# Latent attention with queries and keys made channels-first, and the three passes of a 256-column block in one sum

## The chip, the cores and the metric

The kernel runs on one core of a Trainium2 chip. The metric is the device time of one execution in microseconds (us). TensorE multiplies, VectorE (DVE) and ScalarE (ACT) work element by element, GpSimd (POOL) does a few small things, and the queue of SP issues the loads. Three runs of the kernel before took 1927.31, 1927.44 and 1927.97 us.

## The reference

Two networks run one after the other on 256 tokens of 2048 channels, in float32. The first has two layers, each with a differential attention of 8 heads and a latent attention (MLA) of 8 heads; only the latter is touched. Cut to what matters:

```python
q_b = jnp.einsum('bsr,re->bse', _rms_norm(c_q, mla_q_norm_g[l]), w_uq[l])      # rank 512 -> 8 * (128 + 64)
q_nope, q_rope = q_b[..., :128], q_b[..., 128:]                                # per head
kv = jnp.einsum('bsr,re->bse', _rms_norm(c_kv, mla_kv_norm_g[l]), w_ukv[l])    # rank 512 -> 8 * (128 + 128)
k_nope, v_b = kv[..., :128], kv[..., 128:]
s = (einsum('bqhd,bkhd->bhqk', q_nope, k_nope) + einsum('bqhr,bkr->bhqk', q_rope, k_rope)) * scale
s = jnp.where(dist >= 0, s, NEG_INF); p = softmax(s); o = einsum('bhqk,bkhd->bqhd', p, v_b)
```

## The kernel before

**Products in two parts.** Every weight matrix comes from memory in units of 128 x 1024 numbers (4 KB a partition). ScalarE rounds a unit to its high part (`round_unit`, L393), VectorE takes the rest (`rest_unit`, L398), and TensorE makes three passes for each tile: high by high, high by rest, rest by high. Units go through a ring of four slots; ScalarE and VectorE prepare unit u + 3 in their step u. `product_rows` (L420, passes on L435 to L437) holds a tile of activations (128 channels x 128 tokens) as weights of the array and moves 512 columns of the weight matrix past it, 12 passes a unit; tokens come out on the partitions. `product_cols` (L440), used in the second network only, holds the weight tile and moves tokens: 8 passes of 512 columns (L458, high and rest of the activations side by side) and 8 of 256 (L451).

**Banks.** Sums of a chunk (one block of output columns) lie in a pair of PSUM banks; chunk c uses pair c % 2. `banks_free` (L481) lets TensorE start chunk c when the chunk two before has been copied out, and `evacuated` (L486) lets others wait for that copy. Who copies counts up `acc_free`.

**One layer** has 56 units for q, k, v and gate of the differential attention, then 32 units here called the latent stage (loops at L1261, L1689, L2116), 32 units of the gate of the latent attention (the gate stage, `z_heads`), and 32 of the output matrix. In the latent stage units 0 to 7 and 8 to 15 make the two latents c_q and c_kv (chunks 6 and 7), 16 and 17 the rope key (chunk 8, `product_rope_key`), 18 to 23 the queries (chunks 9 to 11, two units each), 24 to 31 keys and values (chunks 12 to 15).

**Head work is written between the units.** In the latent stage head h of the differential attention has units 4h to 4h + 3: behind unit 4h TensorE turns the weights of the head before (L1115) and q and k of head h (`turn`, L510); behind unit 4h + 1 it multiplies the outputs (L1121 to L1123) and the scores (L1134). ScalarE's list in these steps: copies of the turned weights and of the turned q and k (L1604, L1591), the output of the head (L1611, L1615), the exponentials (L1597). VectorE's list: `diff_max` in step 4h + 1 (L1995 to L2002), `diff_weights` in step 4h + 3 (L2008 to L2014). Every engine works through its list in order, so a wait holds back all that is behind it.

**The latents.** They are scaled by the rms of the tokens and turned to channels-first (`C_TURN`: behind units 10 and 11 for c_q, 18 and 19 for c_kv). ScalarE sums their squares in steps 8 and 16, VectorE makes 1/rms of both by `rsqrt` (eleven small operations, L557 to L562) in step 19, and ScalarE multiplies by it when it copies the products out (L1719). VectorE's `key_sum` (L2119, L2120), at the head of step 18, adds the two halves of the rope key and frees its pair.

**The latent heads** run in the gate stage. Behind unit 4h + 2 TensorE turns the queries and keys without position of head h (`mla_block`, L1167, eight turns of four blocks a layer), ScalarE copies them to `qkT`, and behind unit 4h + 3 `mla_scores` (L1145) multiplies them and adds the rope part. GpSimd rotates the queries' rope part (L1013 to L1019) when chunks 10 and 11 are copied, and TensorE turns it behind the first unit of the gate stage.

## Time and profile before

| what | value |
|---|---|
| median of three runs | 1927.44 us |
| profiled execution | 1927.67 us |
| its span, first to last instruction | 1925.9 us |
| TensorE busy | 1915.0 us, 99% |
| VectorE busy | 1432.9 us, 74% |
| ScalarE busy | 1082.4 us, 56% |
| GpSimd busy | 46.3 us, 2% |
| granted TensorE clock, mean | 0.999 of full speed |

The profiled execution's own time is 1.8 us longer than its span; sums are made against it. Matmuls are pipelined: a pass of 512 columns has a duration of 0.39 us in the list while the next one starts 0.23 us later, so the time that a pass takes up is read from the distance between starts. Layer 0 has its latent stage from about 187 to 287 us and its gate stage from 287 to about 376 us; layer 1 repeats the pattern about 442 us later.

### The profile page before, as it was taken

How to read it: one execution, taken by the hardware profiler on the slowest of the kernel's cores; microseconds unless marked ns; L12 is line 12 of the kernel's file. 1: busy time of each engine (PE TensorE's matmuls, PEld its weight loads, DVE VectorE, ACT ScalarE, POOL GpSimd, SP SyncE). 2: the span in 40 equal slices, each digit the busy share in tenths (PEclk: the TensorE clock that was granted, in tenths of full speed). 3: DMA queues.
4: the chain of work that ended last, by engine and by line, in shares of the span. 5: the costliest groups of instructions: out<-in, count | busy, mean ns of one | idle time of the engine just before them, and what ended most of it. 6: DMA issues, size and time to landing. Idle time of an engine off the chain costs nothing.

```text
span 1925.9 us, 26620 instructions
## 1 busy us (share of the span) xinstructions
PE 1915.0 (99%) x9721; PEld 1624.3 (84%) x9721; DVE 1432.9 (74%) x2059; ACT 1082.4 (56%) x1598; POOL 46.3 (2%) x74
## 2 busy tenths in 40 slices
PE   9999999999999999999999999999999999999998
PEld 7888888888888888888888888888888888888886
DVE  7777675656777675656767766888878887889898
ACT  6555686655545676654644444555555555555554
POOL 1000030000000030000100000000000000000000
PEclk9999999999999999999999999999999999999999
DMA  9864455565665456455666455665666656666664
GB/s 345 309 209 131 147 154 155 152 204 188 209 208 165 141 162 177 142 164 186 210 186 195 154 165 185 185 186 178 203 185 188 192 185 187 191 222 193 203 195 164
DMA packets 248058, 361.29 MB, mean 188 GB/s; under 512 B 15504, under 2 KB 134496, under 8 KB 247456
## 3 DMA queue, kind: packets, MB, share of 16 engines
q1 hardware_dynamic: 246112, 353.15, 58.3%
q0 software_dynamic: 1568, 6.60, 1.0%
q8 instruction: 57, 0.93, 0.2%
q10 hardware_dynamic: 288, 0.33, 0.0%
q14 instruction: 33, 0.27, 0.0%
HBM read 356.88 MB, written 3.16 MB: 187 GB/s over the span
## 4 chain that ended last, share of the span: by engine, by line
PE 97%; DVE 1%; DMA 1%; ACT 0%; issue 0%; SPq 0%; DVEq 0%; ACTq 0%
PE acc L458 22%; PE acc L451 12%; PE acc L435 11%; PE acc L437 11%; PE acc L436 11%; PE acc L1204 4%; PE acc L1205 4%; PE acc L1203 4%; PE acc L1467 3%; PE acc L1465 3%; PE acc L1466 3%; PE aux L515 2%; PE aux L1134 1%; PE aux L1467 1%; PE aux L1465 1%; PE aux L1466 1%
## 5 line engine op out<-in xcount | busy, mean ns | idle before, releaser
L398 DVE TENSOR_TENSOR sb_w_lo<-sb_stage,sb_w_hi 128x1024 fp32r<-128x1024 f32 x476 | 583.1, 1227 | 273.1 <-ACT sb_w_hi L393 266.5
L393 ACT ACTIVATE sb_w_hi<-sb_stage 128x1024 fp32r<-128x1024 f32 x476 | 502.3, 1058 | 349.6 <-PE acc L451 123.0
L458 PE MATMUL acc<-sb_xT,sb_w_hi 128*128 128x512 f32 x1856 | 445.7, 391 | 0.0
L458 PEld LDWEIGHTS acc<-sb_xT,sb_w_hi 128*128 128x128 f32 x1856 | 340.8, 188 | 65.8
L451 PEld LDWEIGHTS acc<-sb_xT,sb_w_lo 128*128 128x128 f32 x1856 | 238.7, 191 | 9.3
L451 PE MATMUL acc<-sb_xT,sb_w_lo 128*128 128x256 f32 x1856 | 243.0, 283 | 0.0
L435 PE MATMUL acc<-sb_w_hi,sb_mT 128*128 128x512 f32 x544 | 217.3, 399 | 0.0
L437 PE MATMUL acc<-sb_w_hi,sb_mT 128*128 128x512 f32 x544 | 212.2, 390 | 0.0
L436 PE MATMUL acc<-sb_w_lo,sb_mT 128*128 128x512 f32 x544 | 212.1, 390 | 0.0
L435 PE MATMUL acc<-sb_w_hi,sb_xT 128*128 128x512 f32 x384 | 155.9, 406 | 0.0
L437 PE MATMUL acc<-sb_w_hi,sb_xT 128*128 128x512 f32 x384 | 150.0, 391 | 0.0
L436 PE MATMUL acc<-sb_w_lo,sb_xT 128*128 128x512 f32 x384 | 149.9, 390 | 0.0
L435 PEld LDWEIGHTS acc<-sb_w_hi,sb_mT 128*128 128x128 f32 x544 | 102.2, 188 | 22.5 <-issue 1.0
L437 PEld LDWEIGHTS acc<-sb_w_hi,sb_mT 128*128 128x128 f32 x544 | 102.2, 188 | 22.0
L436 PEld LDWEIGHTS acc<-sb_w_lo,sb_mT 128*128 128x128 f32 x544 | 102.3, 188 | 19.7
L1203 PE MATMUL acc<-sb_w_hi,sb_xT 128*128 128x512 f32 x220 | 85.7, 389 | 0.0
L1205 PE MATMUL acc<-sb_w_hi,sb_xT 128*128 128x512 f32 x220 | 85.6, 389 | 0.0
L1204 PE MATMUL acc<-sb_w_lo,sb_xT 128*128 128x512 f32 x220 | 85.6, 389 | 0.0
L437 PEld LDWEIGHTS acc<-sb_w_hi,sb_xT 128*128 128x128 f32 x384 | 72.1, 188 | 15.7
L435 PEld LDWEIGHTS acc<-sb_w_hi,sb_xT 128*128 128x128 f32 x384 | 72.2, 188 | 13.9
L738 ACT ACTIVATE sb_w_hi<-sb_pair_stage 128x1024 fp32r<-128x1024 f32 (+1 forms) x50 | 48.3, 982 | 62.2 <-DVE sb_pair_stage L751 53.1
L436 PEld LDWEIGHTS acc<-sb_w_lo,sb_xT 128*128 128x128 f32 x384 | 72.3, 188 | 12.7
(437 smaller groups left out, 2872.6 us busy)
## 6 DMA issues: line engine op xcount, KB each, us to landing
sb_stage<-w_in SPq DMA_DIRECT2D x232, 512.0 KB, 4.1
sb_stage<-w_up SPq DMA_DIRECT2D x176, 512.0 KB, 3.9
sb_stage<-w_out SPq DMA_DIRECT2D x96, 512.0 KB, 4.0
sb_stage<-w_down SPq DMA_DIRECT2D x54, 512.0 KB, 6.8
sb_pair_stage<-w_down SPq DMA_DIRECT2D x34, 512.0 KB, 5.4
sb_kvb<-w_in SPq DMA_DIRECT2D x16, 512.0 KB, 6.2
sb_stage<-w_ukv SPq DMA_DIRECT2D x16, 512.0 KB, 3.8
sb_stage<-w_kv SPq DMA_DIRECT2D x15, 512.0 KB, 6.2
```

What stands on the lines that cost most here:

```text
L393: act.activation(w_hi[:, j % RING, 0:size], stage[:, j % RING, 0:size], ACT.Copy).then_inc(hi_ready, 1)
L398: dve.tensor_tensor(w_lo[:, j % RING, 0:size], stage[:, j % RING, 0:size], w_hi[:, j % RING, 0:size].bitcast(F32), ALU.subtract).then_inc( ...
L435: pe.matmul(o, x_hi, hi[:, k, :], start=first and k == 0, stop=False)
L436: pe.matmul(o, x_hi, lo[:, k, :], start=False, stop=False)
L437: mm = pe.matmul(o, x_lo, hi[:, k, :], start=False, stop=last and k == nk - 1)
L451: mm = pe.matmul(acc[:, 2 * pair + c, 0:SEQ], lo[:, k, c * P:(c + 1) * P], xT[:, k0 + k, 0, :], start=False, stop=False)
L458: mm = pe.matmul(acc[:, 2 * pair + c, :], hi[:, k, c * P:(c + 1) * P], both, start=first and k == 0, stop=last and k == 3)
L1203: pe.matmul(o, a(0), hi, start=start, stop=False)
L1204: pe.matmul(o, a(0), lo, start=False, stop=False)
L1205: return pe.matmul(o, a(1), hi, start=False, stop=stop)
L1465: pe.matmul(o, a(0), hi, start=start, stop=False)
L1466: pe.matmul(o, a(0), lo, start=False, stop=False)
```

## The change

Queries and keys without position are now made channels-first. `w_uq` and `w_ukv` are put together anew on the host, the 128-wide parts of all heads first and the rope or value parts behind them. Units 18 to 21 hold all 512 latent channels by 256 query columns (two heads each), units 24 to 27 the same for keys. The new `product_latent_cols` holds weight tiles and moves the 256 tokens past them: for each of 4 x 2 tiles three passes of 256 columns, all into the same sum. Each of these units is a chunk of its own. Units 22 and 23 make the rope parts of the queries and 28 to 31 the values, as rows, as before.

The turns of the eight latent heads and their copies are gone; `mla_scores` reads the copied chunks. Since tokens no longer lie on the partitions there, 1/rms of c_q goes into the scores' scale (`query_scale`), and c_kv is multiplied by its 1/rms before it is turned (ScalarE, step 18). For that the `rsqrt` stands in VectorE's step 17, and the turns of c_kv behind units 19 and 21. ScalarE copies a column chunk at the head of the step behind it, and the row chunks in steps 24, 30 and the first of the gate stage.

```diff
+DIFF_TB = [2, 3, 4, 7, 8, 10, 12, 13]
+C_TURN = {10: (0, 0, 5), 11: (0, 1, 6), 19: (1, 0, 9), 21: (1, 1, 11)}
...
+QUERY_COLS, KEY_COLS = {18 + n: n for n in range(4)}, {24 + n: n for n in range(4)}
+C_QUERY, C_ROPE, C_KEY, C_VALUE, C_Z, C_OUT = 9, 13, 14, 18, 20, 24
...
+        def product_latent_cols(pe, base, j, k0, pair):
+
+
+            pe.wait_ge(lo_ready, base + (j + 1))
+            hi, lo = (w[:, j % RING, :].rearrange("p (k n) -> p k n", n=256) for w in (w_hi, w_lo))
+            tiles = [(k, c) for k in range(4) for c in range(2)]
+            for k, c in tiles:
+                o, cols = acc[:, 2 * pair + c, 0:SEQ], slice(c * P, (c + 1) * P)
+                pe.matmul(o, hi[:, k, cols], mT[:, k0 + k, 0, :], start=k == 0, stop=False)
+                pe.matmul(o, hi[:, k, cols], mT[:, k0 + k, 1, :], start=False, stop=False)
+                mm = pe.matmul(o, lo[:, k, cols], mT[:, k0 + k, 0, :], start=False, stop=k == 3)
+            mm.then_inc(unit_used, 1)
...
+        query_pair = lambda n: qb[:, n % 2, n // 2 * 512:(n // 2 + 1) * 512].rearrange("p (h t) -> p h t", h=2)
+        key_pair = lambda n: kvb[:, 0, n * 512:(n + 1) * 512].rearrange("p (h t) -> p h t", h=2)
+        query_of, key_of = (lambda h: query_pair(h // 2)[:, h % 2, :]), (lambda h: key_pair(h // 2)[:, h % 2, :])
+        value_of = lambda h, t: kvb[:, 1, t * WIDTH + h * DV:t * WIDTH + (h + 1) * DV]
+        output_of = lambda h, t: kvb[:, 0, h * SEQ + t * DV:h * SEQ + (t + 1) * DV]
+        rope_rows = lambda t: qb[:, t, WIDTH:WIDTH + HEADS * ROPE]
...
-                    for c in range(3):
+                    for n in range(4):
+                        load(sp, base, U_QKV + 18 + n, rows(w_uq, 4, 0, 4, n * 256, 256), 256)
+                    for i in range(2):
+                        load(sp, base, U_QKV + 22 + i, rows(w_uq, 4, i, 2, WIDTH), 512)
+                    for n in range(4):
+                        load(sp, base, U_QKV + 24 + n, rows(w_ukv, 4, 0, 4, n * 256, 256), 256)
+                    for c in range(2):
                         for i in range(2):
-                            load(sp, base, U_QKV + 18 + 2 * c + i, rows(w_uq, 4, i, 2, c * 512), 512)
-                    for c in range(4):
-                        for i in range(2):
-                            load(sp, base, U_QKV + 24 + 2 * c + i, rows(w_ukv, 4, i, 2, c * 512), 512)
+                            load(sp, base, U_QKV + 28 + 2 * c + i, rows(w_ukv, 4, i, 2, WIDTH + c * 512), 512)
...
-                    evacuated(pool, pairs, 10)
-                    evacuated(pool, pairs, 11)
+                    evacuated(pool, pairs, C_ROPE)
...
-                        pe.wait_ge(tb_free, tb0 + (MLA_TB[h] + 1))
+                        if h == 0:
+                            evacuated(pe, pairs, C_KEY + 2)
+                            evacuated(pe, pairs, C_KEY + 3)
+                            pe.wait_ge(tb_free, tb0 + QR_TB + 2)
+                            pe.wait_ge(pv_free, pv0 + 2 * HEADS)
                         pe.wait_ge(row_max, head0 + (HEADS + h))
                         for col, q, keys in ((0, 1, SEQ), (SEQ, 0, P)):
                             o = sc1[:, col:col + keys]
-                            pe.matmul(o, qkT[:, q * P:(q + 1) * P], qkT[:, 2 * P:2 * P + keys], start=True, stop=False)
+                            pe.matmul(o, query_of(h)[:, q * P:(q + 1) * P], key_of(h)[:, 0:keys], start=True, stop=False)
                             mm = pe.matmul(o, qrT[:, h // 2, q * P:(q + 1) * P], krz[:, h % 2, 0:keys],
...
-                            if h < HEADS:
-                                turn(pe, tb0 + MLA_TB[h], mla_block(h))
...
+                        c, i = u // 8, u % 8
+                        if u >= 18:
+                            c, i = C_ROPE - 6, u - 22
+                            if u in QUERY_COLS:
+                                c, i = C_QUERY - 6 + QUERY_COLS[u], 0
+                            if u in KEY_COLS:
+                                c, i = C_KEY - 6 + KEY_COLS[u], 0
+                            if u >= 28:
+                                c, i = C_VALUE - 6 + (u - 28) // 2, u % 2
...
+                        elif u in QUERY_COLS or u in KEY_COLS:
+                            product_latent_cols(pe, base, U_QKV + u, 0 if u < 24 else 4, c % 2)
...
+                            if j == 1:
+                                pe.wait_ge(ckv_scaled, layer + 1)
...
+                    def copy_cols(u, chunk, dst):
+
+                        multiplied(act, quads * 4, U_QKV + u)
+                        pair = chunk % 2
+                        act.activation(dst, acc[:, 2 * pair:2 * pair + 2, 0:SEQ], ACT.Copy).then_inc(acc_free[pair], 1)
+
+                    def copy_rows(u, chunk, dst):
+
+                        multiplied(act, quads * 4, U_QKV + u)
+                        for t in range(T):
+                            ins = act.activation(dst(t), acc[:, 2 * (chunk % 2) + t, :], ACT.Copy)
+                        ins.then_inc(acc_free[chunk % 2], 1)
+
+                    value_rows = lambda c: lambda t: kvb[:, 1, t * WIDTH + c * 512:t * WIDTH + (c + 1) * 512]
+
                     for u in range(32):
+                        if u - 1 in QUERY_COLS:
+                            copy_cols(u - 1, C_QUERY + QUERY_COLS[u - 1], query_pair(QUERY_COLS[u - 1]))
+                        if u - 1 in KEY_COLS:
+                            copy_cols(u - 1, C_KEY + KEY_COLS[u - 1], key_pair(KEY_COLS[u - 1]))
                         rounded(U_QKV + u)
+                        if u == 18:
+                            act.wait_ge(c_rstd, layer + 1)
+                            for t in range(T):
+                                ckv = qb[:, t, RANK:2 * RANK]
+                                ins = act.activation(ckv, ckv, ACT.Copy, scale=rstd_c[:, T + t:T + t + 1])
+                            ins.then_inc(ckv_scaled, 1)
...
-                        if u == 20 or (u > 20 and u % 2 == 1):
-                            c = (u - 19) // 2
-                            act.wait_ge(c_rstd, layer + 1)
-                            multiplied(act, quads * 4, U_QKV + 19 + 2 * c)
-                            for t in range(T):
-                                r = (0 if c < 3 else T) + t
-                                dst = qb[:, t, c * 512:(c + 1) * 512] if c < 3 else \
-                                    kvb[:, t, (c - 3) * 512:(c - 2) * 512]
-                                ins = act.activation(dst, acc[:, 2 * ((9 + c) % 2) + t, :], ACT.Copy,
-                                                     scale=rstd_c[:, r:r + 1])
-                            ins.then_inc(acc_free[(9 + c) % 2], 1)
+                        if u == 24:
+                            copy_rows(23, C_ROPE, rope_rows)
+                        if u == 30:
+                            copy_rows(29, C_VALUE, value_rows(0))
                     for u in range(32):
+                        if u == 0:
+                            copy_rows(31, C_VALUE + 1, value_rows(1))
...
-                        dve.tensor_scalar(s[:, 0:P], sc1[:, 0:P], MLA_SCALE, None, ALU.mult)
-                        two = lambda ap: ap.rearrange("p (m k) -> p m k", m=2)
-                        step(dve.scalar_tensor_tensor(out=two(s[:, P:3 * P]), in0=two(sc1[:, P:3 * P]), scalar=MLA_SCALE,
-                                                      in1=again(causal[:, :], 2), op0=ALU.mult, op1=ALU.add))
+                        dve.scalar_tensor_tensor(out=s[:, 0:SEQ], in0=sc1[:, 0:SEQ], scalar=query_scale[:, 1:2],
+                                                 in1=causal[:, :], op0=ALU.mult, op1=ALU.add)
+                        step(dve.scalar_tensor_tensor(out=s[:, SEQ:SEQ + P], in0=sc1[:, SEQ:SEQ + P],
+                                                      scalar=query_scale[:, 0:1], in1=causal[:, P:2 * P],
+                                                      op0=ALU.mult, op1=ALU.add))
...
-                        if u == 19:
+                        if u in (19, 21):
...
+                        if u == 17:
+                            dve.wait_ge(c_squared, layer * 4 + 4)
+                            rsqrt(step, dve, rstd_c[:, :], sumsq_c[:, :], 4, RANK, done=c_rstd)
+                        if u == 20:
+                            dve.wait_ge(c_rstd, layer + 1)
+                            step(dve.tensor_scalar(query_scale[:, :], rstd_c[:, 0:T], MLA_SCALE, None, ALU.mult))
                         if u % 4 == 1:
                             diff_max(u // 4)
-                        if u == 19:
-                            dve.wait_ge(c_squared, layer * 4 + 4)
-                            rsqrt(step, dve, rstd_c[:, :], sumsq_c[:, :], 4, RANK, done=c_rstd)
...
+    by_part = lambda name, first: np.asarray(arrays[name]).reshape(LAYERS, RANK, HEADS, -1)[:, :, :, first]\
+        .reshape(LAYERS, RANK, -1)
+    data["w_uq"] = np.concatenate([by_part("w_uq", slice(0, NOPE)), by_part("w_uq", slice(NOPE, NOPE + ROPE))], axis=2)
+    data["w_ukv"] = np.concatenate([by_part("w_ukv", slice(0, NOPE)), by_part("w_ukv", slice(NOPE, NOPE + DV))], axis=2)
```

VectorE before, from the rest of unit 20 (step 17, L398) over the scores' maximum of head 4 (L1995 to L2002) to `key_sum` (L2119, L2120) and the rest of unit 21:

```order
L398 TENSOR_TENSOR sb_w_lo<-sb_stage,sb_w_hi 128x1024 [waits hi_ready]
L1995 SCALAR_TENSOR_TENSOR sb_s<-aux,sb_bias 128x512 [waits scores_ready]
L1997 SCALAR_TENSOR_TENSOR sb_s<-aux,sb_bias 128x256
L2000 TENSOR_REDUCE sb_neg_max<-sb_s 128x2 [waits dve_step]
L2001 TENSOR_REDUCE sb_neg_max<-sb_s 128x2
L2002 TENSOR_SCALAR sb_neg_max<-sb_neg_max 128x4 [waits dve_step]
L2119 COPY sb_qb<-acc 128x256 [waits unit_used]
L2120 TENSOR_TENSOR sb_qb<-acc,sb_qb 128x256 [waits dve_step]
L398 TENSOR_TENSOR sb_w_lo<-sb_stage,sb_w_hi 128x1024 [waits hi_ready]
```
VectorE in the changed kernel, the same place (L572 to L577 is the `rsqrt`, L2038 to L2045 the maximum, L2163 and L2164 `key_sum`):

```order
L400 TENSOR_TENSOR sb_w_lo<-sb_stage,sb_w_hi 128x1024 [waits hi_ready]
L572 TENSOR_SCALAR sb_newton_v<-sb_sumsq_c 128x4 [waits c_squared]
...
L577 SCALAR_TENSOR_TENSOR sb_rstd_c<-sb_newton_t,sb_rstd_c 128x4 [waits dve_step]
L2038 SCALAR_TENSOR_TENSOR sb_s<-aux,sb_bias 128x512 [waits scores_ready]
L2040 SCALAR_TENSOR_TENSOR sb_s<-aux,sb_bias 128x256
L2043 TENSOR_REDUCE sb_neg_max<-sb_s 128x2 [waits dve_step]
L2044 TENSOR_REDUCE sb_neg_max<-sb_s 128x2
L2045 TENSOR_SCALAR sb_neg_max<-sb_neg_max 128x4 [waits dve_step]
L2163 COPY sb_qb<-acc 128x256 [waits unit_used]
L2164 TENSOR_TENSOR sb_qb<-acc,sb_qb 128x256 [waits dve_step]
L400 TENSOR_TENSOR sb_w_lo<-sb_stage,sb_w_hi 128x1024 [waits hi_ready]
```
The eleven operations of `rsqrt` have come in between the rest of unit 20 and the maximum, and so ahead of `key_sum`.

ScalarE before, from the exponentials of head 5 (L1597, step 22) on; L393 rounds a unit, L1719 copies queries, L1604 and L1591 are the copies behind unit 24's head work:

```order
L1597 ACTIVATE sb_s,sb_row_sum<-sb_s,sb_neg_max 128x128 x2
L393 ACTIVATE sb_w_hi<-sb_stage 128x1024 [waits unit_used,staged2]
L1719 ACTIVATE sb_qb<-acc,sb_rstd_c 128x512 [waits unit_used,c_rstd]
L1719 ACTIVATE sb_qb<-acc,sb_rstd_c 128x512
L393 ACTIVATE sb_w_hi<-sb_stage 128x1024 [waits unit_used,staged3]
L1604 ACTIVATE sb_pT<-aux 128x384 [waits pv_filled]
L1591 ACTIVATE sb_turn_f<-aux 128x512 [waits tb_filled]
L393 ACTIVATE sb_w_hi<-sb_stage 128x1024 [waits unit_used,staged0]
```
ScalarE in the changed kernel; L1722 copies the rows of units 22 and 23 (chunk 13), L1716 the columns of unit 24:

```order
L1624 ACTIVATE sb_s,sb_row_sum<-sb_s,sb_neg_max 128x128 x2
L395 ACTIVATE sb_w_hi<-sb_stage 128x1024 [waits unit_used,staged2]
L395 ACTIVATE sb_w_hi<-sb_stage 128x1024 [waits unit_used,staged3]
L1631 ACTIVATE sb_pT<-aux 128x384 [waits pv_filled]
L1618 ACTIVATE sb_turn_f<-aux 128x512 [waits tb_filled]
L1722 ACTIVATE sb_qb<-acc 128x512 [waits unit_used]
L1722 ACTIVATE sb_qb<-acc 128x512
L1716 ACTIVATE sb_kvb<-acc 128x512 [waits unit_used]
L395 ACTIVATE sb_w_hi<-sb_stage 128x1024 [waits unit_used,staged0]
```
The copy of units 22 and 23 stood ahead of the rounding in step 23, and now stands behind the two copies that wait for the head work of unit 24.

## Rows read from the trace of the kernel before

**Rows 1.** The page: busy time by engine (share of the span), and the chain's shares
```profile
PE 1915.0 (99%) x9721; PEld 1624.3 (84%) x9721; DVE 1432.9 (74%) x2059; ACT 1082.4 (56%) x1598; POOL 46.3 (2%) x74
...
PE 97%; DVE 1%; DMA 1%; ACT 0%; issue 0%; SPq 0%; DVEq 0%; ACTq 0%
```
**Rows 2.** Timeline of TensorE, a turn alone: start us, duration us, instruction, count
```profile
216.35 0.60 PE L515 MATMUL aux<-sb_ident,sb_qb 128*128 128x128 f32 x4
216.71 0.48 PE L435 MATMUL acc<-sb_w_hi,sb_xT 128*128 128x512 f32 x1
217.03 0.39 PE L436 MATMUL acc<-sb_w_lo,sb_xT 128*128 128x512 f32 x1
```
**Rows 3.** Timeline of TensorE, row products: first and last of 24 passes in a row
```profile
270.58 0.39 PE L435 MATMUL acc<-sb_w_hi,sb_mT 128*128 128x512 f32 x1
...
275.80 0.40 PE L437 MATMUL acc<-sb_w_hi,sb_mT 128*128 128x512 f32 x1
```
**Rows 4.** Timeline of TensorE, a head's turn behind the turn of its weights
```profile
395.05 0.38 PE L515 MATMUL aux<-sb_ident,sb_qb 128*128 128x128 f32 x2
395.27 0.38 PE L515 MATMUL aux<-sb_ident,sb_kvb 128*128 128x128 f32 x2
395.41 0.48 PE L435 MATMUL acc<-sb_w_hi,sb_xT 128*128 128x512 f32 x1
```
**Rows 5.** Timeline of TensorE, column products of the second network's first part
```profile
1244.83 2.08 PE L451 MATMUL acc<-sb_xT,sb_w_lo 128*128 128x256 f32 x16
1246.74 3.82 PE L458 MATMUL acc<-sb_xT,sb_w_hi 128*128 128x512 f32 x16
```
**Rows 6.** The page, weight loads of these 256-column passes: busy us, mean ns
```profile
L451 PEld LDWEIGHTS acc<-sb_xT,sb_w_lo 128*128 128x128 f32 x1856 | 238.7, 191 | 9.3
```
**Rows 7.** Timeline of TensorE, first pass of unit 18 (layer 0)
```profile
239.49 0.50 PE L435 MATMUL acc<-sb_w_hi,sb_mT 128*128 128x512 f32 x1
```
**Rows 8.** Timeline of VectorE, units 17 to 20 of layer 0
```profile
240.44 0.69 DVE L1995 SCALAR_TENSOR_TENSOR sb_s<-aux,sb_bias 128x512 f32<-128x512 f32 x1
...
242.62 0.42 DVE L2119 COPY sb_qb<-acc 128x256 f32<-128x256 f32 x1
...
243.41 1.22 DVE L398 TENSOR_TENSOR sb_w_lo<-sb_stage,sb_w_hi 128x1024 fp32r<-128x1024 f32 x1
...
250.00 0.16 DVE L557 TENSOR_SCALAR sb_newton_v<-sb_sumsq_c 128x4 f32<-128x4 f32 x1
...
252.05 1.22 DVE L398 TENSOR_TENSOR sb_w_lo<-sb_stage,sb_w_hi 128x1024 fp32r<-128x1024 f32 x1
```
**Rows 9.** Timeline of ScalarE, the last of the exponentials of head 4
```profile
244.43 0.19 ACT L1597 ACTIVATION_READ_ACCUMULATOR sb_s<-sb_s,sb_neg_max 128x1 f32 x1
```
**Rows 10.** Timeline of TensorE, head work behind unit 24, and unit 25
```profile
262.60 0.49 PE L1115 MATMUL aux<-sb_ident,sb_s 128*128 128x128 f32 x3
...
263.28 0.48 PE L435 MATMUL acc<-sb_w_hi,sb_mT 128*128 128x512 f32 x1
```
**Rows 11.** Timeline of ScalarE, the copies of that head, and of a chunk
```profile
263.12 0.49 ACT L1604 ACTIVATE sb_pT<-aux 128x384 f32<-128x384 f32 x1
...
264.06 1.05 ACT L393 ACTIVATE sb_w_hi<-sb_stage 128x1024 fp32r<-128x1024 f32 x1
...
268.49 1.27 ACT L1719 ACTIVATE sb_kvb<-acc,sb_rstd_c 128x512 f32<-128x512 f32 x2
...
269.64 1.07 ACT L393 ACTIVATE sb_w_hi<-sb_stage 128x1024 fp32r<-128x1024 f32 x1
```
**Rows 12.** Timeline of GpSimd, first and last operation of the queries' rotation
```profile
262.40 1.53 POOL L1013 TENSOR_TENSOR sb_kz<-sb_qb,sb_rope 128x512 f32<-128x512 f32 x1 [0.90 <-ACT sb_qb L1719]
...
273.68 0.80 POOL L1019 TENSOR_TENSOR sb_kz<-sb_kz 128x256 f32<-128x256 f32 x1
```
**Rows 13.** Timeline of TensorE, the start of the program
```profile
1.02 5.06 PE L1050 MATMUL acc<-sb_turn_f 128*128 128x128 f32 x22 [1.02 <-POOL sb_turn_f L960]
...
5.82 1.19 PE L1060 MATMUL acc<-sb_w_hi,sb_mT 128*128 128x512 f32 x2
```

More of the change, by code:

```diff
@@ L79 @@
 N_FFN = D_FF // 256
-C_MEM, C_LAYER = 2, 24
+C_MEM, C_LAYER = 2, 28
 G_NORM = 0
@@ L223, in shape_constants @@
     q, k = np.arange(P)[:, None], np.arange(P)[None, :]
-    causal = np.where(q - k >= 0, 0.0, NEG).astype(np.float32)
+    causal = np.concatenate([np.zeros((P, P)), np.where(q - k >= 0, 0.0, NEG)], axis=1).astype(np.float32)
     inv = (1.0 / (THETA ** (np.arange(0, ROPE, 2, dtype=np.float32) / ROPE))).astype(np.float32)
@@ L1177, in gated_block @@
                             return lambda i: qa[:, t, (4 * g + i) * DV:(4 * g + i + 1) * DV]
-                        v = lambda i: (4 * (g - 2) + i) * (NOPE + DV)
-                        return lambda i: kvb[:, t, v(i):v(i) + DV]
+                        return lambda i: output_of(4 * (g - 2) + i, t)
                     def z_heads(u):
                         h, r = (u - 2) // 4, (u - 2) % 4
-                        if u >= 2 and r == 0:
-                            if 0 < h <= HEADS:
-                                mla_turn_weights(h - 1)
-                            if h < HEADS:
-                                turn(pe, tb0 + MLA_TB[h], mla_block(h))
+                        if u >= 2 and r == 0 and 0 < h <= HEADS:
+                            mla_turn_weights(h - 1)
                         if u >= 2 and r == 1:
@@ L1627, in mla_output @@
                         act.wait_ge(pv_filled, pv0 + (2 * HEADS + 2 * h + 2))
-                        v = h * (NOPE + DV)
                         for t, col, r in ((1, 0, 0), (0, P, 1)):
-                            ins = act.activation(kvb[:, t, v:v + DV], pv[:, col:col + P], ACT.Copy,
+                            ins = act.activation(output_of(h, t), pv[:, col:col + P], ACT.Copy,
                                                  scale=inv_sum[:, r:r + 1])
@@ L1636, in z_heads @@
                         h, r = (u - 2) // 4, (u - 2) % 4
-                        if u >= 2 and r == 0:
-                            if 0 < h <= HEADS:
-                                copy_weights(2 * HEADS + 2 * (h - 1))
-                            if h < HEADS:
-                                copy_bank(MLA_TB[h], qkT)
+                        if u >= 2 and r == 0 and 0 < h <= HEADS:
+                            copy_weights(2 * HEADS + 2 * (h - 1))
                         if u >= 2 and r == 1 and 0 < h <= HEADS:
@@ L2042, in gate_outputs @@
                             dve.wait_ge(pv_free, layer * (4 * HEADS) + (2 * HEADS + 8 * (g - 1)))
-                            o = kvb[:, t, :].rearrange("p (h e) -> p h e", h=HEADS)[:, 4 * (g - 2):4 * (g - 1), 0:DV]
+                            o = kvb[:, 0, :].rearrange("p (h t d) -> p h t d", h=HEADS, t=T)[:, 4 * (g - 2):4 * (g - 1), t, :]
                         dve.tensor_tensor(o, o, z, ALU.mult).then_inc(gated, 1)
```

59 lines of the change are left out of this document (24 added, 35 removed).

## The prediction

> **What bounds the kernel now.** I read the page first. TensorE is busy 99% of the span and carries 97% of the chain that ended last [rows 1]. So nothing that only VectorE, ScalarE or GpSimd does costs time, unless it makes TensorE wait; and every pass that TensorE is spared or given counts in full. I then took the timeline of TensorE through one layer, to price a pass and a turn by the distance between starts (durations overlap, so a row's duration is no price), and the timelines of VectorE and ScalarE around the latent units, to see when each sum is copied out of its pair of banks. In the document's numbering the stage has units 0 to 31. Both layers show the same pattern, so I work out layer 0 and double.
>
> **Turns removed.** Eight turns of four 128-column passes go per layer. A turn standing alone: start at 216.35, next product at 216.71, and that product's first pass takes 0.32 to the next start where 0.227 is usual [rows 2, 3]. That is 0.36 + 0.09 = 0.45 us. Seven of the eight stand behind the turn of a head's weights, whose tail is paid anyway; they give 395.05 to 395.41 = 0.36 us each [rows 4]. Together 0.45 + 7 x 0.36 = 2.97 us a layer. One of the two turns of the normalized key latent moves from behind unit 18 to behind unit 21, where scores stand before it: another 0.09. What they removed on ScalarE (a copy per head) was hidden under TensorE's products and gives nothing.
>
> **Passes.** A row product has 12 passes of 512 columns, a unit of the new kind 24 of 256: the same columns, twice the instructions. 512 columns: 23 distances from 270.58 to 275.80, 0.227 each [rows 3], so 2.72 us a unit. 256 columns, each with weights of its own, stand in the mixer's column products: 16 from 1244.83 to 1246.74, 0.1194 each [rows 5], so 2.87 us a unit. The price is 0.14 us for each of eight units, 1.1 us a layer. Bounds: half of 0.227 would make it nothing; if a weight load, 191 ns long in its rows [rows 6], could not lie under the pass before it, a unit would take 24 x 0.191 = 4.58, 1.86 more. I take 0.1194, since in rows 5 the weights change at every pass as here. Not shown there is three passes in a row into the same 256 columns of a bank; the 512-column passes of rows 3 do that without a gap, so I add nothing.
> The Trainium skill, "TensorE: Matmul & The Clock Gate", says under "The mechanism" (Part 3) that a weight load overlaps a running matmul only where the row groups differ. By that rule every one of these passes would pay its load; rows 5 and 6 contradict it (16 starts in 1.91 us with loads of 191 ns), and the measurement decides.
>
> **First new wait: unit 19 for the sum of the rope key.** This is where I expect the saving to go. Each query block is now a chunk of its own, so unit 18 takes pair 1 and unit 19 already pair 0, in which the rope key of units 16 and 17 lies until VectorE's key_sum has read it. Before, pair 0 was wanted only by unit 20. At the same time the rsqrt of the latents is moved ahead of diff_max(4) and key_sum on VectorE (the order shown in the section on the change).
> Without a wait unit 19 would start at 239.49 [rows 7] + 0.09 tail + 2.87 = 242.45. VectorE is through with the rest of unit 20 at 240.44. The rsqrt takes 250.00 to 252.05, 2.05 us, so 242.49. diff_max(4) took 240.44 to 242.62, 2.18, so 244.67. key_sum took 242.62 to 243.41, 0.79, so 245.46 [rows 8]. TensorE then loads weights, 0.19 [rows 6], and starts at 245.65. A wait of 3.2 us per layer. Behind it stand the turn of the key latent, unit 20 and head 4's weights; none has another way past. What is late next: ScalarE's exponentials of head 4 wait for diff_max, and the copy that frees pair 1 for unit 20 stands behind them. They ended at 244.43 + 0.19, 2.0 after diff_max [rows 8, 9]; so now at 246.7, and with half of a chunk's 1.15 [rows 11] the copy at 247.3. Unit 20 wants it at 245.65 + 2.87 + 0.36 = 248.9. No wait there.
>
> **Second new wait: unit 25 for the rope part of the queries.** Units 22 and 23 are a row chunk in pair 1, unit 24 a chunk in pair 0, and unit 25 wants pair 1 again. The copy of units 22 and 23 stands on ScalarE behind unit 24's head work: the copy of the turned weights and the copy of the turned q and k, both of which wait for TensorE after unit 24. From rows: TensorE's head work behind unit 24 began at 262.60, the next product at 263.28; ScalarE had both copies done at 264.06, that is 1.46 after the head work began. The two 512-column copies of a chunk took 268.49 to 269.64, 1.15 [rows 10, 11]. So the pair is free 2.61 after the head work's start, with a weight load 2.80, where unit 25 would start at 0.68: 2.1 us a layer. This one doesn't depend on how late anything runs before, since ScalarE waits for TensorE itself and TensorE for ScalarE.
>
> **What else moves.** GpSimd starts the queries' rotation after that copy instead of after the one at 262; it took 262.40 to 273.68 + 0.80 [rows 12] and is wanted only behind the first unit of the gate stage, which begins at 287, so even 7 us later it is hidden. Scaling the key latent on ScalarE (two copies) comes before head 4's exponentials, which wait longer for diff_max anyway: nothing. The two operations of mla_max become two others of like size, the loads have the same bytes in other blocks; SP issues as many, and nothing waits for a load: nothing. The copy of the first value chunk now stands behind head 7's exponentials and is wanted by the first unit of the gate stage; I take nothing for it and put up to 1 us on the upper side, together with the slowing of VectorE beside GpSimd's rotation.
>
> **Sum.** Per layer: -2.97 - 0.09 + 1.1 + 3.2 + 2.1 = +3.4 us. Twice: +6.8. The profiled execution took 1927.67 (span 1925.9, 1.8 around it), which makes 1934.5; it lies 0.23 above the median of the runs, so in their terms 1934.2. I forecast 1934.4, slower by 0.36%.
>
> **Rivals.** A difference under 0.2% (3.9 us) can't be told from none here.
> - The saving stands and the waits do not: another release comes earlier than I read. -2.97 - 0.09 + 1.1 = -1.9 a layer, 1923.6, which is at the edge between "same" and "faster". For it: TensorE hardly ever waits before. Against: both waits follow from the order on a single queue. With only the first wait left it would be 1930, with only the second 1927.9. 8% for none, 8% for one.
> - TensorE's clock falls in the gaps. The granted clock is at full speed in all 40 slices of before, and no gap of 3 us stands in the trace after the start. At the start, behind idle time, 22 passes of 128 columns took from 1.02 to 5.82, 0.218 each, where two such passes now take 395.05 to 395.27, 0.110 each: 2.4 us lost [rows 4, 13]. If that came once per layer, 1939.2. 8%. The Trainium skill, the same page, "What's actually happening", says that the array's clock is at half by default and released by activity, so that idle time lets it fall again; no row here shows it behind a gap like this one.
> - Passes of 256 columns cost the length of a weight load: 16 x 1.86 = 29.8 in place of 2.3 makes 1962. 3%.
> The forecast has 73%, with a range of its own from 1932 to 1937. Taking in one lost wait and the clock, the range is 1929.8 to 1939.8. Slower: 73 + 8 + 3, less 2 for a forecast that comes out smaller than the bound, 0.82. The 8 for one wait, those 2 and 2 of the 8 for none are same, 0.12; the other 6 are faster, 0.06.
>
> **What will show it.** In the profile after: TensorE idle for about 3.2 us ahead of the first 256-column pass of the second query block in each layer, released by VectorE's key_sum, and about 2.1 us ahead of the second key block, released by ScalarE's copy; both in the list of waits as two occurrences each. The turn group of qb and kvb has 64 fewer passes. 24 starts of the new line in 2.87 us. The gate stage is shorter by about 3 us a layer. I am wrong if TensorE's idle time stays near 2 us, if the granted clock shows less than full speed in the slices of the latent units, or if the new passes start over 0.125 apart.

## The result, and the profile after

| | median, us | runs | range, us |
|---|---|---|---|
| before | 1928.13 | 6 | 1927.31 to 1930.62 |
| after | 1936.70 | 6 | 1935.77 to 1937.65 |

The ratio is 1.0043, with a 95% interval of 1.0032 to 1.0054: slower, as forecast, and 2.3 us above the forecast time. The profiled execution took 1936.7 us with a span of 1934.9, 9.0 more than the one of before.

Look first at the list of what TensorE waited for. Its columns are engine and line, the releaser, then us in total, times, and the longest.

```profile
PE acc L480 <- DVE sb_qb L2164: 6.0, 2, 3.0
PE acc L480 <- ACT sb_qb L1722: 3.3, 2, 1.7
PE acc L1551 <- DVE sb_w_lo L767: 1.2, 1, 1.2
```

L480 is the first pass of a block of query or key channels. L2164 is VectorE's key_sum and L1722 is ScalarE's copy of units 22 and 23. Both waits are the forecast ones, once per layer each. The third is at the very end of the program, where before it showed 0.3 (there the line is L1524).

The page says the same of the whole: TensorE is still busy 99% of the span, but its part of the chain that ended last fell from 97% to 94% and VectorE's rose to 3%, answering to [rows 1].

```profile
PE 1913.7 (99%) x9849; PEld 1628.4 (84%) x9849; DVE 1433.8 (74%) x2061; ACT 1074.9 (56%) x1586; POOL 47.3 (2%) x74
...
PE 94%; DVE 3%; ACT 1%; DMA 1%; issue 1%; SPq 0%; ACTq 0%; DVEq 0%
```

TensorE's timeline in layer 0, first passes of unit 18, its last shown pass, and the start of unit 19 (start us, duration us, instruction, count, idle time before it and its releaser):

```profile
239.66 0.39 PE L480 MATMUL acc<-sb_mT,sb_w_hi 128*128 128x256 f32 x1
239.88 0.28 PE L481 MATMUL acc<-sb_mT,sb_w_hi 128*128 128x256 f32 x1
...
242.40 0.28 PE L481 MATMUL acc<-sb_mT,sb_w_hi 128*128 128x256 f32 x1
242.52 0.28 PE L482 MATMUL acc<-sb_mT,sb_w_lo 128*128 128x256 f32 x1
245.79 0.39 PE L480 MATMUL acc<-sb_mT,sb_w_hi 128*128 128x256 f32 x1 [2.99 <-DVE sb_qb L2164]
...
266.62 0.54 PE L1138 MATMUL aux<-sb_ident,sb_s 128*128 128x128 f32 x3
...
269.26 0.39 PE L480 MATMUL acc<-sb_mT,sb_w_hi 128*128 128x256 f32 x1 [1.67 <-ACT sb_qb L1722]
```

The new passes start 0.12 apart. Unit 19 could have started at 242.64 and starts at 245.79: 3.15 us. The head work behind unit 24 starts at 266.62 and unit 25 only 2.64 later, where it was 0.68 in [rows 10]: 1.96 us. The bracket shows less than the start-to-start loss, because it counts idle time from the modelled end of the last pass. Distances between starts are what the kernel pays.

VectorE ahead of unit 19 shows why: the rsqrt, diff_max(4) and key_sum stand one behind the other.

```profile
240.63 0.16 DVE L572 TENSOR_SCALAR sb_newton_v<-sb_sumsq_c 128x4 f32<-128x4 f32 x1
...
242.69 0.68 DVE L2038 SCALAR_TENSOR_TENSOR sb_s<-aux,sb_bias 128x512 f32<-128x512 f32 x1
...
244.86 0.42 DVE L2163 COPY sb_qb<-acc 128x256 f32<-128x256 f32 x1
...
245.65 1.22 DVE L400 TENSOR_TENSOR sb_w_lo<-sb_stage,sb_w_hi 128x1024 fp32r<-128x1024 f32 x1
```

Key_sum is through at 245.65, read as in [rows 8] by the start of the operation behind it; the forecast had 245.46 and unit 19 at 245.65.

**Where the 9.0 us are.** I compare the starts of the head work (L1115 before, L1138 after). From the one behind unit 16 to the one behind the first unit of the gate stage, layer 0 took 54.21 us before (235.25 to 289.46) and takes 60.47 now (235.44 to 295.91): +6.26. The two waits are 5.11 of it, eight units at 0.14 are 1.14, the moved turn gives 0.04 back, together 6.21. From there to the last head's weights it was 118.93 and is 115.71: -3.22, the turns. (These weights are turned behind the third unit of the output stage. The gate stage itself runs from 286.7 to 400.1 us in the kernel before, not to 376.) So layer 0 pays 3.04. Layer 1 pays 3.05 of the same kind and 1.49 more, because there TensorE's clock fell. The wait at the very end is 0.9 longer. That is 8.5 of 9.0. Of the rest, 0.19 in each layer lie between the head work behind unit 4 and that behind unit 16 (40.30 us before, 40.49 now). TensorE has the same 211 passes and turns there in both kernels, but 116 of the row passes start 229.7 ns apart on average where it was 227.8.

The clock in layer 1, by stretches of 1 us (stretch, length, busy time and count of TensorE, its weight loads, VectorE, ScalarE and GpSimd, granted clock, DMA share, GB/s):

```profile
689.00:690.00 1.00, 0.00 (x0) 0.00 (x0) 0.96 (x4) 0.15 (x2) 0.00 (x0) 1.00 0.00 0
690.00:691.00 1.00, 0.25 (x2) 0.25 (x3) 0.97 (x3) 1.00 (x5) 0.00 (x0) 1.00 0.00 0
691.00:692.00 1.00, 1.00 (x8) 1.00 (x8) 0.99 (x2) 1.00 (x6) 0.00 (x0) 0.73 0.00 0
692.00:693.00 1.00, 1.00 (x7) 1.00 (x6) 0.93 (x4) 1.00 (x2) 0.00 (x0) 0.50 0.06 15
...
694.00:695.00 1.00, 1.00 (x7) 1.00 (x7) 0.00 (x0) 0.00 (x0) 0.00 (x0) 0.56 0.62 204
695.00:696.00 1.00, 1.00 (x11) 1.00 (x10) 0.14 (x1) 0.00 (x0) 0.00 (x0) 1.00 0.00 0
```

TensorE was idle for 3.0 us up to 690.75. About 0.7 us after it went on, the granted clock fell to 0.50, which is the lower of its two levels (1.2 GHz), and came back before 695. The passes between stand 0.21 apart instead of 0.12 (692.49, 692.70, 692.91, 693.13 in the timeline). In the 40 slices of the page nothing of it can be seen: every slice of the granted clock still shows 9, that is 90% or more.

### The profile page after: what moved, and what is told of

Read it like the earlier page. It is cut to its first block, busy times and chain, and to the rows that moved or that the text cites. A ratio compares the mean times of both kernels' runs of the same rounds, so it can differ in the third digit from the quotient of the medians.

```text
span 1934.9 us, 26850 instructions
## 1 busy us (share of the span) xinstructions
PE 1913.7 (99%) x9849; PEld 1628.4 (84%) x9849; DVE 1433.8 (74%) x2061; ACT 1074.9 (56%) x1586; POOL 47.3 (2%) x74
## 4 chain that ended last, share of the span: by engine, by line
PE 94%; DVE 3%; ACT 1%; DMA 1%; issue 1%; SPq 0%; ACTq 0%; DVEq 0%
PE acc L460 22%; PE acc L453 11%; PE acc L437 10%; PE acc L439 10%; PE acc L438 10%; PE acc L1221 4%; PE acc L1223 4%; PE acc L1222 4%; PE acc L1492 2%; PE acc L1493 2%; PE acc L1494 2%; PE aux L530 1%; PE aux L1492 1%; PE aux L1493 1%; PE aux L1494 1%
## 5 line engine op out<-in xcount | busy, mean ns | idle before, releaser
L437 PE MATMUL acc<-sb_w_hi,sb_mT 128*128 128x512 f32 x480 | 191.3, 399 | 0.0
L438 PE MATMUL acc<-sb_w_lo,sb_mT 128*128 128x512 f32 x480 | 187.2, 390 | 0.0
L439 PE MATMUL acc<-sb_w_hi,sb_mT 128*128 128x512 f32 x480 | 187.2, 390 | 0.0
L437 PEld LDWEIGHTS acc<-sb_w_hi,sb_mT 128*128 128x128 f32 x480 | 90.2, 188 | 19.8 <-issue 1.0
L439 PEld LDWEIGHTS acc<-sb_w_hi,sb_mT 128*128 128x128 f32 x480 | 90.2, 188 | 19.5
L438 PEld LDWEIGHTS acc<-sb_w_lo,sb_mT 128*128 128x128 f32 x480 | 90.3, 188 | 17.5
```

Of the source, the lines that this page charges most:

```text
L437: pe.matmul(o, x_hi, hi[:, k, :], start=first and k == 0, stop=False)
L438: pe.matmul(o, x_hi, lo[:, k, :], start=False, stop=False)
L439: mm = pe.matmul(o, x_lo, hi[:, k, :], start=False, stop=last and k == nk - 1)
```

## The experiments

All expected times are set against the kernel before at about 1928 and the changed one at 1936.7.

**1. The key_sum first.** On VectorE, ahead of the rsqrt instead of behind diff_max(4):

```diff
-                        if u == 18:
-                            multiplied(dve, base, U_QKV + 17)
-                            step(dve.tensor_copy(key_sum, acc[:, 0, SEQ:2 * SEQ]))
-                            dve.tensor_tensor(key_sum, acc[:, 0, 0:SEQ], key_sum, ALU.add).then_inc(acc_free[0], 1)
...
                         if u == 17:
+                            multiplied(dve, base, U_QKV + 17)
+                            step(dve.tensor_copy(key_sum, acc[:, 0, SEQ:2 * SEQ]))
+                            dve.tensor_tensor(key_sum, acc[:, 0, 0:SEQ], key_sum, ALU.add).then_inc(acc_free[0], 1)
                             dve.wait_ge(c_squared, layer * 4 + 4)
```

> One edit against the changed kernel: on VectorE the key_sum stands ahead of the rsqrt of the latents, so pair 0 comes free at about 241.4 instead of 245.65 in layer 0. My theory: unit 19 no longer waits (3.15 us a layer, and in layer 1 the fall of the clock behind that gap, 1.5 us, goes too). But diff_max(4) still ends at 245.65, ScalarE's exponentials of head 4 at 247.6, and the copy that frees pair 1 behind them at 248.2; unit 20, which now wants pair 1 at about 245.9, waits for it 2.4 us. So only 0.8 a layer comes back, and the clock's 1.5 only if a gap of 2.4 leaves it alone: 1936.7 - 1.6 - 1.5 = 1933.6 (1935.1 with the clock's loss). Rival A, nothing is late next: 1936.7 - 6.3 - 1.5 = 1928.9. Rival B, unit 19 waits for something other than the key_sum: 1936.7.

Measured: 1933.66 (7 runs, 1932.62 to 1934.11), ratio to before 1.0029 (1.0018 to 1.0040). My theory had 1933.6. Unit 19 starts without a wait, and the wait comes up again at unit 20. TensorE and ScalarE of this kernel:

```profile
245.82 0.60 PE L530 MATMUL aux<-sb_ident,sb_qb 128*128 128x128 f32 x4
248.46 0.39 PE L480 MATMUL acc<-sb_mT,sb_w_hi 128*128 128x256 f32 x1 [2.04 <-ACT sb_qb L1716]
```

```profile
247.74 0.19 ACT L1624 ACTIVATION_READ_ACCUMULATOR sb_s<-sb_s,sb_neg_max 128x1 f32 x1
247.83 0.57 ACT L1716 ACTIVATE sb_qb<-acc 128x512 f32<-128x512 f32 x1
```

The copy that frees pair 1 stands behind the last exponential of head 4. One move on VectorE only handed the wait from pair 0 to pair 1. The granted clock stayed at 1.00 behind this gap in both layers.

**2. The copy of unit 18 first as well.** On ScalarE, in step 18 before the exponentials of head 4 instead of at the head of step 19:

```diff
-                        if u - 1 in QUERY_COLS:
+                        if u - 1 in QUERY_COLS and u > 19:
...
                             ins.then_inc(ckv_scaled, 1)
+                            copy_cols(18, C_QUERY, query_pair(0))
```

> As the run with key_sum first, and on ScalarE the copy of the first query block (unit 18) stands ahead of the exponentials of head 4 instead of behind them. It is done at about 245.2, before unit 20 wants the pair at 245.9. My theory: both the wait of unit 19 and the one behind it are gone, with the clock's 1.5: 1936.7 - 6.3 - 1.5 = 1928.9. The weights of head 4 are ready at about 249.0, when TensorE wants to turn them at 248.9: at most 0.2 a layer more. Rival: the exponentials, later by 0.6, hold TensorE at the turn of head 4's weights by 1 us or more: 1931 or above. If the waits were not the price, no change: 1936.7.

Measured: 1930.55 (11 runs, 1929.84 to 1931.77), ratio 1.0013 (1.0004 to 1.0022). Between theory and rival, 1.6 above the theory. The wait of unit 19 and the one of unit 20 are gone, and another stood behind them: unit 21 waits for the copy of unit 19.

```profile
PE acc L480 <- ACT sb_qb L1722: 3.3, 2, 1.7
...
PE acc L480 <- ACT sb_qb L1716: 1.0, 2, 0.5
```

It costs 0.73 from start to start, in each layer (from head 4's weights to unit 21 it is 1.75 here and 1.01 in experiment 5, where this wait is gone), which is nearly all of the 1.6. ScalarE did that copy only behind the rounding of the turned key latent, and the rounding waits for VectorE:

```profile
250.30 0.63 ACT L548 ACTIVATE sb_mT<-sb_turn_f 128x512 fp32r<-128x512 f32 x1 [0.94 <-DVE sb_turn_f L541]
250.84 0.58 ACT L1716 ACTIVATE sb_qb<-acc 128x512 f32<-128x512 f32 x1
```

**3. The copy of units 22 and 23 first,** alone, against the changed kernel:

```diff
+                        if u == 24:
+                            copy_rows(23, C_ROPE, rope_rows)
                         rounded(U_QKV + u)
...
-                        if u == 24:
-                            copy_rows(23, C_ROPE, rope_rows)
```

> One edit against the changed kernel: on ScalarE the copy of units 22 and 23 (the rope part of the queries) stands ahead of what follows unit 24's head work, not behind it. My theory: unit 25 starts 0.7 after the head work's start as in the kernel before, where it stood at 2.64; 1.96 us a layer come back: 1936.7 - 3.9 = 1932.8, and the first wait and the clock's fall in layer 1 stay. Rival: the pair is held by something else, or VectorE's rounding is what unit 25 waits for next: 1936.7, or above 1934.

Measured: 1933.86 (6 runs, 1932.95 to 1936.11), ratio 1.0033 (1.0020 to 1.0045). The second wait is gone:

```profile
266.65 0.54 PE L1138 MATMUL aux<-sb_ident,sb_s 128*128 128x128 f32 x3
...
267.38 0.36 PE L480 MATMUL acc<-sb_mT,sb_w_hi 128*128 128x256 f32 x1
```

0.73 from head work to unit 25. The whole kernel came out 1 us above the expectation. In the profiled execution the clock's fall in layer 1 was longer than in the changed kernel's (at 0.50 for 6.8 us and not 3.4) and cost 2.6 instead of 1.5 (the distance from head work to head work around unit 19 is 19.23 there and 16.63 where the clock holds).

**4. All three moves.**

> All three moves together (key_sum first, the copies of unit 18 and of units 22 and 23 first): what the change itself gives without its two waits. From the terms of the prediction: before (1928.1) - 2 x 1.9 = 1924.3; from the trace after: 1936.7 - 6.3 - 1.5 - 3.9 = 1925.0. So 1924.6, faster than before by 0.18%. If the two waits were only part of what slowed the kernel (passes of 256 columns, the exponentials), it stays at or above 1928.

Measured: 1927.06 (11 runs, 1925.10 to 1930.06), ratio 0.9997 (0.9988 to 1.0006): no different from before, 2.5 above what I expected. 1.5 of that is the wait of unit 21 that experiment 2 shows and that the expectation did not have. Another 0.6 is lost at the turn of head 4's q and k, which experiment 5 shows alone.

**5. A fourth move: the copy of unit 19 first.** On ScalarE, ahead of the rounding of the turned key latent:

```diff
-                        if u - 1 in QUERY_COLS and u > 19:
+                        if u - 1 in QUERY_COLS and u > 20:
...
+                        if u == 19:
+                            copy_cols(19, C_QUERY + 1, query_pair(1))
                         if u in C_TURN:
```

> The kernel with all three moves (1927.06) and one more: on ScalarE the copy of the second query block (unit 19) stands ahead of the rounding of the turned key latent, which waits for VectorE. My theory: there unit 21 started at 250.49 where it could have at 249.7, so 0.8 us a layer comes back: 1925.5, 0.13% faster than before. If the exponentials or the rounding of weights behind the copy become late instead, nothing comes back: 1927.0. If the long tail there is something else, no change either.

Measured: 1925.17 (11 runs, 1924.13 to 1926.73), ratio 0.9985 (0.9976 to 0.9994). As the theory had it, and the only version with the whole result that is faster than the kernel before, by 0.15%, less than the 0.2% that I count as a difference, though the interval lies wholly below 1. No L480 stands in its list of waits any more:

```profile
PE acc L1073 <- POOL sb_turn_f L985: 1.0, 1, 1.0
PE acc L1100 <- ACT sb_w_hi L395: 0.8, 1, 0.8
PE acc L1551 <- DVE sb_w_lo L767: 0.5, 1, 0.5
```

One delay is left in the latent stage, and it is too short for that list. TensorE at head 4 (weights, q and k, unit 21), and VectorE:

```profile
248.95 0.55 PE L1138 MATMUL aux<-sb_ident,sb_s 128*128 128x128 f32 x3
249.55 0.44 PE L530 MATMUL aux<-sb_ident,sb_qa 128*128 128x128 f32 x2
...
249.96 0.36 PE L480 MATMUL acc<-sb_mT,sb_w_hi 128*128 128x256 f32 x1
```

```profile
248.81 0.68 DVE L541 TENSOR_TENSOR sb_turn_f<-aux,sb_gain_c 128x512 f32<-128x512 f32 x1
```

From the weights to unit 21 it is 1.01, where it was 0.68 before and in the changed kernel (252.07 to 252.75). The turn of q and k goes to the bank with the key latent turned behind unit 19, and VectorE reads that only behind the arithmetic on head 4's weights, until 249.49. With the 0.10 that the weights themselves are late this is 0.43 a layer.

**6. Wide passes.** From here on "four moves" is the kernel of experiment 5. In its product of latent columns, the two passes with the weights' high part become one of 512 columns, whose second half goes to the other half of the bank and is not copied out, so the product of high weights and low activations is missing from the result:

```diff
-                pe.matmul(o, hi[:, k, cols], mT[:, k0 + k, 0, :], start=k == 0, stop=False)
-                pe.matmul(o, hi[:, k, cols], mT[:, k0 + k, 1, :], start=False, stop=False)
-                mm = pe.matmul(o, lo[:, k, cols], mT[:, k0 + k, 0, :], start=False, stop=k == 3)
+                both = mT[:, k0 + k, :, :].rearrange("p h t -> p (h t)")
+                pe.matmul(acc[:, 2 * pair + c, :], hi[:, k, c * P:(c + 1) * P], both, start=k == 0, stop=False)
+                mm = pe.matmul(acc[:, 2 * pair + c, 0:SEQ], lo[:, k, c * P:(c + 1) * P], mT[:, k0 + k, 0, :],
+                               start=False, stop=k == 3)
```

> As the kernel with four moves, but a unit of query or key blocks is 8 passes of 512 columns and 8 of 256 instead of 24 of 256. The product of the weights' high part with the activations' low part then lies in the other half of the bank and is left out of the result; the columns that TensorE passes are the same. By the rows, 8 x 0.227 + 8 x 0.12 = 2.78 against 2.88 us a unit: 0.10 x 16 units, 1.7 us less than the kernel with four moves, 1923.8. Rival, the cost goes by columns alone: no change. Rival, the weight load paces the 256-column passes where another pass of 256 stands next to it: more than 3 us less.

Measured: 1925.48 (11 runs, 1924.55 to 1926.77), against 1925.17 with narrow passes: no gain. My 1.7 us fell for two reasons. A pass of 512 and one of 256 take 0.353 together, not 0.347:

```profile
240.56 0.39 PE L480 MATMUL acc<-sb_mT,sb_w_hi 128*128 128x512 f32 x1
240.79 0.28 PE L481 MATMUL acc<-sb_mT,sb_w_lo 128*128 128x256 f32 x1
240.91 0.40 PE L480 MATMUL acc<-sb_mT,sb_w_hi 128*128 128x512 f32 x1
```

So a unit is shorter by 0.05 and not by 0.10. And what it gains is waited away. For the stretch from the head work behind unit 16 to the one behind the first unit of the gate stage, TensorE of layer 0 needs 55.79 us here and 55.85 with narrow passes, where eight units should have given 0.4. From the last pass of unit 20 to the weights of head 4 it is 0.39 here, 0.22 with narrow passes, and 0.12 would be a pass (249.00 to 249.39, and 248.73 to 248.95, in the two timelines). Those weights are the end of a chain through VectorE and ScalarE that faster passes do not shorten. Two smaller delays of the same kind take the rest: 0.07 ahead of head 5's weights, and 0.19 ahead of unit 28, which starts at 275.36 when ScalarE has copied unit 26 at 275.31.

**7. The turns put back,** into the kernel with four moves:

```diff
+                        if u >= 2 and r == 0 and h < HEADS:
+                            pe.wait_ge(tb_free, tb0 + QR_TB + 2 + sum(g < u for g in GATE_TURN))
+                            for i in range(4):
+                                pe.transpose(aux[:, 0, i * P:(i + 1) * P], ident[:, :], ident[:, :])
```

> As the kernel with four moves, with the eight turns of a latent head's blocks put back into the gate stage as four 128-column passes each on data at hand, behind the same kind of wait and used by nobody. My theory of what the change gives: 0.45 + 7 x 0.36 = 2.97 a layer by the prediction, 3.22 a layer by the distances of the two traces; so 6.0 to 6.4 more than the kernel with four moves, 1931.5 to 1931.9. Rival, the turns are partly hidden and the gate stage became shorter through something else (the copy per head on ScalarE): under 4 more.

Measured: 1932.20 (11 runs, 1931.38 to 1933.01) against 1925.17: 7.0 us, 3.5 a layer, above both my figures. A head's weights in the kernel with four moves, and the same place with the turns back:

```profile
393.75 0.49 PE L1138 MATMUL aux<-sb_ident,sb_s 128*128 128x128 f32 x3
393.99 0.48 PE L437 MATMUL acc<-sb_w_hi,sb_xT 128*128 128x512 f32 x1
```

```profile
396.85 0.49 PE L1138 MATMUL aux<-sb_ident,sb_s 128*128 128x128 f32 x3
397.18 0.60 PE L1210 MATMUL aux<-sb_ident 128*128 128x128 f32 x4
397.53 0.47 PE L437 MATMUL acc<-sb_w_hi,sb_xT 128*128 128x512 f32 x1
```

0.24 from the weights to the next product without the turn and 0.68 with it: a turn costs 0.44 behind weights too, not the 0.36 from its own start to the next instruction's. The part that I took for a tail paid anyway, 0.33 up to the turn instead of 0.24, is paid only when a turn follows. The rival is out: the copy per head on ScalarE stays away here, and the cost is over 4.

**8. A longer gap.** The changed kernel with four more copies ahead of the key_sum:

```diff
-                            step(dve.tensor_copy(key_sum, acc[:, 0, SEQ:2 * SEQ]))
+                            for _ in range(5):
+                                step(dve.tensor_copy(key_sum, acc[:, 0, SEQ:2 * SEQ]))
```

> The changed kernel with four more copies of 256 columns (0.45 us each) ahead of the key_sum on VectorE, so that TensorE's gap before unit 19 is 4.8 us instead of 3.0. If the gap costs its length alone: 2 x 1.8 = 3.6 more, 1940.3. My theory: the clock, which fell behind the gap of 3.0 in layer 1 and not in layer 0, falls in both now, so layer 0 pays 1.5 more and layer 1 as much again as before or more: 1941.8 to 1944. Rival, the fall in layer 1 has to do with the place and not with the gap: 1940.3, and layer 0 at full speed.

Measured: 1941.98 (5 runs, 1940.59 to 1942.72), ratio 1.0070 (1.0057 to 1.0084). This is at the lower end of my theory, and above the rival's 1940.3. The gap is 4.8 us, and now the clock falls in layer 0 as well as in layer 1:

```profile
244.00:246.00 2.00, 0.00 (x0) 0.00 (x0) 1.90 (x6) 1.15 (x4) 0.00 (x0) 1.00 0.01 4
246.00:248.00 2.00, 0.04 (x1) 0.04 (x1) 1.86 (x6) 2.00 (x8) 0.00 (x0) 0.94 0.00 0
248.00:250.00 2.00, 2.00 (x9) 2.00 (x10) 1.93 (x5) 0.61 (x1) 0.00 (x0) 0.50 0.00 0
250.00:252.00 2.00, 2.00 (x15) 2.00 (x14) 0.16 (x1) 0.00 (x0) 0.00 (x0) 0.71 0.84 262
252.00:254.00 2.00, 2.00 (x20) 2.00 (x19) 1.02 (x2) 0.29 (x1) 0.00 (x0) 1.00 0.00 0
```

**9 and 10. The changed kernel once more, and a gap in between** (three copies in place of five above), one execution each.

> The changed kernel as it is, once more, to see whether the fall of the clock behind the 3.0 us gap belongs to layer 1 or comes by chance. So far, with the same gap, layer 1 fell in two profiles of two and layer 0 in none of two. If it belongs to the place: layer 1 falls again and layer 0 does not, 1936 to 1938. If it is by chance: any other pattern is as likely as this one (layer 0 falls, or neither does; with neither 1935.2). What it costs is 1.5 to 2.5 each.

> The changed kernel with two more copies of 256 columns (0.45 us each) ahead of the key_sum, so a gap of 3.9 us instead of 3.0, between the two lengths of which one showed a fall in one layer of two and the other in both. If the gap costs its length alone: 1936.7 + 1.8 = 1938.5. My theory, that a longer gap makes the fall likelier: both layers fall, 1940 to 1941; with only one falling, 1938.5.

Measured: 1937.7 and 1939.76, the second a little under my 1940 to 1941. In both the clock fell in both layers. Layer 0 of the changed kernel, which had kept its clock in the first profile, this time:

```profile
244.00:246.00 2.00, 0.00 (x0) 0.00 (x0) 1.90 (x6) 1.15 (x4) 0.00 (x0) 1.00 0.02 8
246.00:248.00 2.00, 1.76 (x9) 1.76 (x10) 1.92 (x5) 2.00 (x9) 0.00 (x0) 0.62 0.00 0
248.00:250.00 2.00, 2.00 (x12) 2.00 (x11) 0.55 (x2) 0.72 (x1) 0.00 (x0) 0.53 0.77 252
250.00:252.00 2.00, 2.00 (x20) 2.00 (x19) 0.65 (x2) 0.00 (x0) 0.00 (x0) 1.00 0.03 10
```

So the fall does not belong to layer 1. My expectation for the repeat, that only layer 1 falls, had the wrong pattern, and the rival by chance stands: the same kernel with the same gap kept its clock in layer 0 in one execution and lost it in another.

## Why the prediction was right, point by point

- **The mechanism.** Both waits arose at the forecast places with the forecast releasers: 3.15 against 3.2 us, and 1.96 against 2.1. Experiments 1 to 5 take them away and get back what they cost, 1936.7 to 1925.2. This is shown.
- **Nothing late behind the first wait.** True as the change orders the work. Experiment 1 shows on what it rests: the exponentials have to follow diff_max closely, and once the key_sum goes first the same copy is 2.0 us late.
- **Passes.** 0.14 a unit, as forecast: 24 starts 119.7 ns apart against 12 starts 227.7 ns apart. The trace has no sign of a weight load that isn't covered: the passes start 0.12 apart while a load of L480 to L482 takes 197 ns (191 in [rows 6]). The rule of the Trainium skill, "TensorE: Matmul & The Clock Gate", section "The mechanism" (Part 3), that a load overlaps a matmul only where the row groups differ, is contradicted here a second time, if it is taken alone. The same section also lets a load for a background weight buffer be pulled ahead of running matmuls; the trace agrees that loads lie under running passes, and cannot show in which buffer. If every load had been paid, the kernel would have stood at 1962.
- **The turns were mis-sized.** The step "whose tail is paid anyway; they give 0.36 us each" failed: a turn is 0.44 (experiment 7), so eight give 3.5 a layer and not 2.97. From before to after the stretch of the latent heads became shorter by 3.22 only. What is given back is in the row products: 360 of their passes start 227.9 ns apart before, 362 start 228.9 ns apart now, in both layers and in every version of the changed kernel, which is 0.37 a layer. Why they stand one nanosecond further apart no run here shows. The moved turn was mis-sized too, 0.04 and not 0.09: it takes 0.41 behind the scores of unit 21.
- **Sum per layer.** +3.04 in layer 0 against +3.4. That it came out so near is in part luck: per layer the turns gave 0.53 more than forecast and the two waits cost 0.2 less, while the row passes took 0.4 back there and 0.2 ahead of unit 16, which stood at nothing in the sum. At nothing in it stood also, for the whole kernel, the clock's 1.5 and the 0.9 of the wait at the end.
- **The clock was a rival at 8% and came true in part.** I had priced it at 2.4 us in each layer, from the program's start [rows 13]. In the profiled execution it fell in one layer and cost 1.5; in the repeated one it fell in both. The step that failed is that I weighed it as all or nothing for both layers, on the argument that no such gap stands in the trace of before. That no gap of 3 us was to be seen there was no evidence that the clock would hold through one. The Trainium skill says in the same page, "What's actually happening", that the clock is at half by default and released by activity. The traces agree in the direction, with 0.50 behind eight of ten gaps of 3.0 us and more, but behind two gaps of 3.0 it stayed at 1.00.
- **The rest,** 0.9 us of a longer wait at the very end (L1551), is no part of the change as far as these runs show: the same wait is 0.3 in the repeated run of the changed kernel and 0.9 in the one of experiment 8.

With the waits gone, the sum of the terms (8 turns at 0.44, 8 units at 0.14, the moved turn at 0.04) is -2.4 a layer, or 1923.3, and the kernel with four moves takes 1925.2. The two traces show where the 1.9 lie: per layer 0.43 at head 4 (experiment 5), 0.37 in the row passes of the latent heads' stretch, 0.19 in those between units 4 and 16, together 1.0. What stays open is why those row passes stand further apart; that the turns put back leave them at 228.9 ns shows only that it isn't the turns' absence.

## What to carry to other kernels

When a change cuts an accumulated sum into more chunks that take turns in two pairs of banks, count for each chunk which instruction frees the pair and what stands ahead of it on its engine's queue. Here the removed turns saved 7 us and the waits in the queues took 10 back. They could be undone by moving an operation a few places up in its queue, but behind unit 19's wait stood unit 20's, behind that one unit 21's, and a delay of 0.43 us a layer at head 4 is still there. Price a removed instruction by the distance between its neighbours with it and without it, not by its own start to the next.

## What the runs showed of the hardware that was not expected

The clock of TensorE fell to 0.50 behind idle gaps in the middle of a busy program, and not in every execution; what decides it, these runs don't show. Over all profiles of these kernels, per layer: behind gaps of 1.7 us (12 of them) and of 2.0 us (2) never, behind 3.0 us in four of six, behind 3.9 in two of two, behind 4.8 in two of two. The fall cost 1.4 to 2.6 us each time, taken as the distance between the head work ahead of the gap and the one behind it, less 16.63 and less what the gap was lengthened by. It also came at different moments: in experiment 3 the clock was down before TensorE went on (0.50 from 688 on, unit 19 at 688.96), in the profile after 0.7 us behind it. So a gap of 3 us costs its length and on average about another microsecond, an estimate from four falls of 1.5 to 2.6 in six gaps.
